# Twenty-four value rows gathered as half rows, and the last gate layer split by input half

## The chip, the core and the metric

The kernel runs on one core of a Trainium2 chip. It is one program with one instruction stream for each engine: TensorE (PE, and PEld for its weight loads), VectorE (DVE), ScalarE (ACT), GpSimd (POOL) and the DMA queue of SyncE (SP). Engines wait for one another through semaphores. The metric is the device time of one execution in microseconds (us), as the median of several runs.

## What is computed

Two transformer blocks on 256 tokens of width 2048, in float32. The change lies at the very end of the second block: a feed-forward layer that looks up experts in a table, and after it a gate layer.

```
def peer_ffn(x, w_peer_q, peer_subkeys, peer_u, peer_v):
    ...                       # per token: 8 heads x 16 experts of 16384, softmax gates
    def chunk(args):          # 128 tokens
        xc, ec, gc = args
        u = peer_u[ec]
        act = jax.nn.gelu(jnp.einsum('tkd,td->tk', u, xc))
        return jnp.einsum('tk,tkd->td', gc * act, peer_v[ec])
...
    h = h + peer_ffn(rms_norm_2(h, ffn_norm[l]), ...)
    gate = jax.nn.sigmoid(rms_norm_2(h, ple_norm[l]) @ w_ple_gate[l])
    h = h + gate * (p[l] @ w_ple_proj[l])
return rms_norm_2(h, final_norm)
```

Each token needs 128 rows of `peer_u` and 128 rows of `peer_v`, 2048 floats each. For the 256 tokens that is 512 gathers, each of one row for 128 tokens (1 MiB).

## The kernel before

**Gathers.** The list `gathers` holds one entry for each transfer: `("u", n, k)` or `("v", n, k)`, where n is token half times 8 plus head (0 to 15) and k the expert (0 to 15). GpSimd issues them in this order as indirect DMAs (L640), each into one of ten row buffers `ROWS`: four in `BIG`, one in `HF`, five in `HLF`, which later hold the split weights of the gate layer. A gather waits until its buffer's last row was used (L629 to L633). The transfers number from q = 0 to 511; u rows run ahead of v rows, the last u row is q = 494.

**Use of a row.** VectorE takes every u row (a dot product with the normed input, L2730). Of the v rows TensorE takes three of four: ScalarE makes a diagonal matrix of the row's gates (`DIAG`), and TensorE multiplies it with the row's four blocks of 512 columns and sums in four banks. VectorE takes the fourth (multiply and add into `ACC`, L2750). Eight rows of the last head (n = 15, k from 8 on) are cut between them: VectorE takes the left 1024 columns (L2746), TensorE the right ones.

**From sums to the gate layer.** After the last row VectorE adds a bank into `ACC` (`joined`, 512 columns), TensorE turns that block (`turned_values`, four transposes), VectorE adds it to the residual X (`added`), ScalarE squares it (`half_square`) and makes the upper half of the normed input (four chunks of 128), and VectorE makes the lower half (`normed_low`). This goes block by block, four blocks of 512 columns for the second 128 tokens.

**The gate layer** `w2_pg` has 32 units of 512 KiB, two for each of 16 output chunks of 128 columns: one for the input's left 1024 columns, one for the right. A unit is loaded by SP into one of three `RAW` buffers, copied with rounding by ScalarE (`high`), and its remainder made by VectorE (`low`), into one of five `HLF` buffers; then TensorE makes 24 products of 256 columns. `RAW` is free again after `low`. For a finished chunk VectorE multiplies the bank with the row norm `RX` (`scaled`, into `GT`), ScalarE takes the sigmoid in place, VectorE multiplies with `PRJ` and adds to X, and ScalarE squares it and scales it for the output (`OUT`). There are three banks for the chunks.

VectorE's order in this layer is written out in its `dense`: for each unit `low(u + 3)`, and after a chunk's last unit the four steps above. Every engine works strictly in the order of its own stream.

Of the kernel before, what the change touches and what calls it, by code (L numbers as in the profile page):

```python
# [7 lines left out]
U32 = mybir.dt.uint32  # L8
# [35 lines left out]
          ("w2_pg", 16, 8, 128, 2, False)]  # L44
# [3 lines left out]
LATE = ("w_ck", "w_out", "w2_ao", "w2_pg")  # L48
# [140 lines left out]
def build(nc, A, out):  # L189
    ctx = ExitStack()  # L190
    with ctx:
# [9 lines left out]
        STREAM = [A[n[:5]][int(n[5:])] if n[:5] in ("w2_uk", "w2_uv") else A[n][b * a.parts + p]  # L201
# [132 lines left out]
        ROWS = [big(12288 + 2048 * i, 2048) for i in range(4)] + [HF[:, 0, 0:2048]] + [HLF[:, i, :] for i in range(NPAIR)]  # L334
        DIAG = [KEEP[:, i // 2, 128 * (i % 2):128 * (i % 2) + 128] for i in range(4)]
# [18 lines left out]
        us, vs = [[(x, n, k) for n in range(16) for k in range(16)] for x in ("u", "v")]  # L354
        gathers = []
        for a in range(256):
            gathers.append(us[a])
            while vs and a >= 16 * vs[0][1] + 17 and 256 - len(vs) < min((a - 17) * 240 / 238, (a - 39) * 1.6):
                gathers.append(vs.pop(0))
        gathers += vs  # L360
        taken = {g: q for q, g in enumerate(gathers)}

        def by_vector(g):
            return g[0] == "u" or g[2] % 4 == 3 or (g[1] == 15 and g[2] % 2 == 1)

        def halved(g):

            return g[0] == "v" and g[1] == 15 and g[2] >= 8

# [9 lines left out]
        last = [3, pair[2], pair[3], 4, 0, 1, 2, 3, pair[2], pair[3]]  # L379
        NG = len(gathers)  # L380

        def buffer(q):
            if q < 19:
                return first_rows[q]
            if q < 46:
                return beside_pq[(q - 19) % 9]
            return early[(q - 16) % 10] if q < NG - 10 else last[q - NG + 10]

        place, used, vturn, pturn, seen = [], [[] for _ in ROWS], [], [], [0, 0]
        for q, g in enumerate(gathers):  # L390
            b = buffer(q)
            place.append((b, len(used[b]) + 1, used[b][-1] if used[b] else None))
            used[b].append(q)
            seen[0] += not by_vector(g) or halved(g)
            seen[1] += by_vector(g) or halved(g)
# [3 lines left out]
        PG_FREE = max(used[b][-1] for b in (pair[4], pair[0], pair[1]))  # L399
# [10 lines left out]
        s_row = [sem(f"rows{i}_in") for i in range(5 + NPAIR)]  # L410
# [35 lines left out]
        s_sig, s_res = sem("ple_sigmoid"), sem("ple_added")  # L446
# [37 lines left out]
        PQ0, PP0, PG0 = L["w_pq"].unit0, L["w2_pp"].unit0, L["w2_pg"].unit0  # L484
# [79 lines left out]
        def gpsimd(e):  # L564
# [59 lines left out]
            for q, (table, n, k) in enumerate(gathers):  # L624
# [4 lines left out]
                if before is not None:  # L629
                    if by_vector(gathers[before]) or halved(gathers[before]):  # L630
                        e.wait_ge(s_vused, vturn[before])
                    if not by_vector(gathers[before]) or halved(gathers[before]):
                        e.wait_ge(s_pused, pturn[before])  # L633
# [4 lines left out]
                elif slot == 4:  # L638
                    e.wait_ge(s_mm, L["w_pq"].end())
                e.indirect_dma_start(out=ROWS[slot], out_offset=None, in_=A["peer_" + table],  # L640
# [7 lines left out]
        def tensor(e):  # L648
# [605 lines left out]
            def value(q, n, k, table="v"):  # L1254
# [13 lines left out]
                for b in range(2 if halved((table, n, k)) else 0, 4):  # L1268
                    end = 14 if i == 0 else 6 if b < 2 else 15
                    m = mm(PS[4 - 4 * i + b][:, :], DIAG[(p - 1) % 4], ROWS[slot][:, 512 * b:512 * b + 512], n % 8 + k == 0,  # L1270
                           n % 8 == 7 and k == end)
                m.then_inc(s_pused, 1)

            def turned_values(i, j):
                pe.wait_ge(s_acc, 4 * i + 4 if i == 0 else 5 + j)
                if i == 1 and j < 2:
# [14 lines left out]
            for q, (table, n, k) in enumerate(gathers):  # L1291
                if not by_vector(gathers[q]) or halved(gathers[q]):
                    value(q, n, k)
# [20 lines left out]
            dense(L["w2_pg"], normed("ple_norm"), None, None, later_sums)  # L1314
# [9 lines left out]
        def scalar(e):  # L1324
# [629 lines left out]
            for q, (table, n, k) in enumerate(gathers):  # L1954
# [6 lines left out]
                if not by_vector(gathers[q]) or halved(gathers[q]):  # L1961
# [7 lines left out]
                if q == PG_FREE + 5:  # L1969
                    s.wait_ge(s_vused, max(vturn[p] for p in range(PG_FREE + 1)))  # L1970
                    s.wait_ge(s_pused, max(pturn[p] for p in range(PG_FREE + 1)))
                    for j in range(3):
                        high(L["w2_pg"].unit0 + j)
            pg = L["w2_pg"]
            s.wait_ge(s_vused, VTURNS)
            s.wait_ge(s_pused, PTURNS)
            high(pg.unit0)
            high(pg.unit0 + 1)
            for j in range(4):
                if j == 2:  # L1980
                    high(pg.unit0 + 2)
# [8 lines left out]
            def evac_pg(c):  # L1990
                bank_done(L["w2_pg"], c)
# [7 lines left out]
            high(pg.unit0 + 3)  # L1999
            high(pg.unit0 + 4)  # L2000
            dense(pg, evac_pg)
# [5 lines left out]
        def vector(e):  # L2007
# [676 lines left out]
            def route(n):  # L2684
# [31 lines left out]
                ts(GA[:, i, 16 * h:16 * h + 16], BV, BV[:, 0:1], None, ALU.subtract)  # L2716
                copy(EX[:, i, 16 * h:16 * h + 16], I12[:, 0:16], (s_ext, n + 1))
# [22 lines left out]
            def value(q, n, k):  # L2740
# [3 lines left out]
                if halved(("v", n, k)):  # L2744
                    o = ACC[:, i, 0:1024]
                    v.done(e.scalar_tensor_tensor(out=o, in0=row[:, 0:1024], scalar=c, in1=o, op0=ALU.mult, op1=ALU.add), sig)  # L2746
# [6 lines left out]
            def joined(i, b):  # L2753

                v.wait_ge(s_pused, pturn[taken["v", 8 * i + 7, 14 if i == 0 else 6 if b < 2 else 15]])
                o = ACC[:, i, 512 * b:512 * b + 512]
                tt(o, o, PS[4 - 4 * i + b][:, :], ALU.add, (s_acc, 4 * i + b + 1))
# [244 lines left out]
```

## Time and profile before

| | |
|---|---|
| median of 3 runs | 3695.53 us (3695.16 to 3697.79) |
| profiled execution, its own time | 3696.61 us |
| its span, first to last instruction | 3694.8 us |
| busy: PE, DVE, ACT, POOL | 87%, 68%, 39%, 24% of the span |
| DMA moved | 952.30 MB, mean 258 GB/s |

The span is what the rows of the trace cover; the execution's own time is 1.8 us more, and the median of the runs 0.7 us more than the span. All times in rows count from the start of the span. The last gather lands in the last 120 us of the span, and everything the change touches lies in the last 200 us.

### The profile page before, as it was taken

The numbers are of one execution on the slowest core, as the hardware profiler recorded it, in microseconds if no ns is written. First come the engines' busy times: TensorE is split into PE (matmuls) and PEld (weight loads), VectorE is DVE, ScalarE is ACT, GpSimd is POOL, SyncE is SP. The second block draws the span as 40 slices with busy tenths as digits, with TensorE's granted clock in tenths as the row PEclk, the third lists the DMA queues.
The fourth block names the chain that finished last, engine by engine and source line by source line (L and its number), as shares of the span: only waits on it lengthen the run. The fifth ranks groups of instructions, "written<-read, shape, count | busy, mean of one in ns | idle before, by whom it ended". The sixth has DMA issues, their size and how long they took to land.

```text
span 3694.8 us, 44301 instructions
## 1 busy us (share of the span) xinstructions
PE 3200.4 (87%) x16462; PEld 2476.9 (67%) x16462; DVE 2496.8 (68%) x3435; ACT 1429.4 (39%) x2139; POOL 899.5 (24%) x624
## 2 busy tenths in 40 slices
PE   8998999999999999999999999677666666666678
PEld 7777878888888889998998888533222232222248
DVE  6578866665566567875647766966777786555566
ACT  6455655653355445565546551211100110100125
POOL 2000010000000100000000013565655566566522
PEclk9998999999999999999999999898988888878799
DMA  6433343556555555455553458999999999999974
GB/s 217 159 123 115 107 161 127 183 188 195 182 190 192 191 203 187 161 184 192 177 177 115 158 187 323 417 422 421 421 421 422 421 421 422 422 421 421 422 282 160
DMA packets 187879, 952.30 MB, mean 258 GB/s; under 512 B 20880, under 2 KB 21008, under 8 KB 121872
## 3 DMA queue, kind: packets, MB, share of 16 engines
q0 software_dynamic: 73728, 536.90, 35.0%
q1 hardware_dynamic: 113936, 412.56, 33.9%
q8 instruction: 131, 2.15, 0.2%
q14 instruction: 84, 0.69, 0.1%
HBM read 947.29 MB, written 2.10 MB: 257 GB/s over the span
## 4 chain that ended last, share of the span: by engine, by line
PE 57%; DMA 21%; DVE 14%; POOL 3%; ACT 3%; issue 2%; DVEq 0%; ACTq 0%; SPq 0%; POOLq 0%
PE ps L658 56%; DMA HLF<-in_peer_v,CS 9%; DMA BIG<-in_peer_v,CS 6%; DMA HLF<-in_peer_u,CS 3%; DVE HL L2027 2%; DVE HLF L2730 2%; DMA HF<-in_peer_v,CS 2%; DVE BIG L2031 1%; POOL BIG L640 1%; POOL HLF L640 1%; DVE BIG L2027 1%; DVE BIG L2730 1%; DMA BIG<-in_peer_u,CS 1%; ACT HL L1343 1%; DVE BIG L2023 1%
## 5 line engine op out<-in xcount | busy, mean ns | idle before, releaser
L658 PE MATMUL ps<-HS,HL 128*128 128x256 f32 (+1 forms) x7040 | 1110.2, 314 | 0.0
L2027 DVE TENSOR_TENSOR HL<-RAW,HL 128x1024 fp32r<-128x1024 f32 (+1 forms) x736 | 905.8, 1231 | 233.9 <-ACT HL L1343 175.2
L658 PEld LDWEIGHTS ps<-HS,HL 128*128 128x128 f32 x7040 | 992.9, 192 | 83.0 <-issue 2.9
L1343 ACT CAST HL<-RAW 128x1024 fp32r<-128x1024 f32 (+1 forms) x736 | 768.5, 1044 | 463.4 <-PE ps L658 178.7
L658 PE MATMUL ps<-BIGR,HL 128*128 128x256 f32 (+1 forms) x5376 | 888.7, 320 | 14.4 <-ACT HL L1343 9.5
L658 PEld LDWEIGHTS ps<-BIGR,HL 128*128 128x128 f32 x5376 | 779.4, 192 | 92.8 <-issue 11.7
L658 PE MATMUL ps<-HLF,KEEP 128*128 128x512 f32 x724 | 386.0, 687 | 193.4 <-DMA HLF<-in_peer_v,CS 177.0
L658 PE MATMUL ps<-BIG,KEEP 128*128 128x512 f32 x648 | 336.4, 672 | 164.2 <-DMA BIG<-in_peer_v,CS 126.4
L658 PEld LDWEIGHTS ps<-HLF,KEEP 128*128 128x128 f32 x724 | 155.1, 222 | 421.6 <-issue 353.9
L2730 DVE CUSTOM_DVE_ANT_0 HLF<-HLF,BIG 128x2048 f32<-128x2048 f32 x133 | 304.9, 2293 | 191.2 <-DMA HLF<-in_peer_u,CS 183.2
L658 PEld LDWEIGHTS ps<-BIG,KEEP 128*128 128x128 f32 x648 | 135.6, 217 | 360.0 <-issue 331.5
L1339 ACT ACTIVATE KEEP<-CON,GA 128x128 f32<-128x128 f32 x192 | 77.1, 402 | 729.4 <-PE ps L658 642.1
L576 POOL COPY NSUM<-TMP 128x256 f32<-128x256 f32 x5 | 3.5, 692 | 1459.3 <-ACT TMP L1339 1459.3
L2730 DVE CUSTOM_DVE_ANT_0 BIG<-BIG 128x2048 f32<-128x2048 f32 x97 | 222.4, 2293 | 117.4 <-DMA BIG<-in_peer_u,CS 110.8
L640 POOL DMA_INDIRECT HLF<-in_peer_u,CS x133 | 207.2, 1558 | 97.8 <-PE ps L658 49.4
L640 POOL DMA_INDIRECT HLF<-in_peer_v,CS x124 | 180.6, 1457 | 169.7 <-PE ps L658 124.6
L640 POOL DMA_INDIRECT BIG<-in_peer_v,CS x111 | 153.8, 1386 | 147.4 <-PE ps L658 116.7
L578 POOL TENSOR_TENSOR NSUM<-NSUM,TMP 128x256 f32<-128x256 f32 x74 | 92.3, 1248 | 344.0 <-ACT TMP L1339 342.9
L640 POOL DMA_INDIRECT BIG<-in_peer_u,CS x97 | 148.9, 1535 | 95.9 <-DVE CS L2035 33.4
L2027 DVE TENSOR_TENSOR X<-X,ps 128x256 f32<-128x256 f32 (+1 forms) x168 | 72.9, 434 | 143.1 <-PE ps L658 137.4
L658 PE MATMUL ps<-HL,HS 128*128 128x512 f32 x576 | 137.6, 396 | 0.2 <-ACT BIG L1339 0.2
L658 PEld LDWEIGHTS ps<-HL,HS 128*128 128x128 f32 x576 | 107.6, 190 | 25.0 <-issue 2.3
(219 smaller groups left out, 2550.5 us busy)
## 6 DMA issues: line engine op xcount, KB each, us to landing
RAW<-in_w_up SPq DMA_DIRECT2D x128, 512.0 KB, 3.5
RAW<-in_w_down SPq DMA_DIRECT2D x128, 512.0 KB, 4.2
RAW<-in_w_out SPq DMA_DIRECT2D x64, 512.0 KB, 3.4
RAW<-in_w_qk SPq DMA_DIRECT2D x32, 512.0 KB, 3.7
RAW<-in_w_xbc SPq DMA_DIRECT2D x32, 512.0 KB, 3.2
RAW<-in_w_xr SPq DMA_DIRECT2D x32, 512.0 KB, 3.4
RAW<-in_w_yr SPq DMA_DIRECT2D x32, 512.0 KB, 3.3
RAW<-in_w_gr SPq DMA_DIRECT2D x32, 512.0 KB, 3.9
```

Of the source, the lines that this page charges most:

```text
L576: g.done(e.tensor_copy(NSUM[:, :], sq[:, 0, :]), sig)
L578: g.done(e.tensor_tensor(NSUM[:, :], NSUM[:, :], sq[:, j, :], ALU.add), sig)
L640: e.indirect_dma_start(out=ROWS[slot], out_offset=None, in_=A["peer_" + table], in_offset=bass.IndirectOffsetOnAxis(ap=EX[:, i, 16 * h + k ...
L658: return e.matmul(o, l, r, start=start, stop=stop, skip_group_check=True)
L1339: s.done(e.activation(o, i, f, bias=bias, scale=scale), sig)
L1343: s.done(e.copy(o, i), sig)
L2023: v.done(e.tensor_scalar(o, i, s1, s2, op0, op1), sig)
L2027: v.done(e.tensor_tensor(o, a, b, op), sig)
L2031: v.done(e.scalar_tensor_tensor(out=o, in0=a, scalar=s, in1=b, op0=op0, op1=op1), sig)
L2730: v.done(e.tensor_tensor_reduce(row, row, HN[:, i, :], 1.0, 0.0, ALU.mult, ALU.add, DOT[:, i, 16 * h + k:16 * h + k + 1]), sig)
```

## The change

The 24 v rows (n = 14, k from 8) and (n = 15, all k) are no longer gathered whole. They leave the list of whole rows, which then ends at q = 487, and follow it as 24 left halves ("l", 512 KiB each) and then 24 right halves ("r"). The index of a half row is twice the expert's, plus one for a right half; VectorE makes both lists in the routing step (four small operations for each of two heads). The halves go into ten half buffers, two in each of the four `BIG` rows and the `HF` row, in turn. TensorE takes the left halves with even k and VectorE the others; VectorE takes all right halves.

The gate layer becomes two layers of 16 units, `w2_pg0` (left inputs) and `w2_pg1` (right inputs). `w2_pg0` starts when the left half of X is complete; ScalarE copies its 16 results into `GSUM`. VectorE meanwhile adds right halves and makes lows by turns. When all right halves are added, the right half of X is completed, and `w2_pg1` runs. For each chunk VectorE now adds bank and `GSUM`, multiplies with `RX`, and goes on as before.

```
-          ("w2_pg", 16, 8, 128, 2, False)]
+          ("w2_pg0", 16, 8, 128, 1, False), ("w2_pg1", 16, 8, 128, 1, False)]
...
+        split = [(n, k) for n in (14, 15) for k in range(16) if n == 15 or k >= 8]
+        vs = [x for x in vs if x[1:] not in split]
...
+        NF = len(gathers)
+        gathers += [(x, n, k) for x in ("l", "r") for n, k in split]
...
+            if q < NF:
+                return early[(q - 16) % 10]
+            return 10 + 2 * ((q - NF) % 5) + (q - NF) // 5 % 2
```

On TensorE:

```
-            for j in range(4):
-                turned_values(1, j)
-            half_sum(1, 0)
-            half_sum(1, 1)
+            turned_values(1, 0)
+            turned_values(1, 1)
...
-            dense(L["w2_pg"], normed("ple_norm"), None, None, later_sums)
+            gated = normed("ple_norm")
+            dense(L["w2_pg0"], gated, None, None, first_sums)
+            turned_values(1, 2)
+            turned_values(1, 3)
+            dense(L["w2_pg1"], lambda k: gated(k + 8), None, None, later_sums)
```

On ScalarE:

```
+            def evac_first(c):
+                s.wait_ge(s_mm, L["w2_pg0"].done(c))
+                copy(GSUM[:, c, :], bank(L["w2_pg0"], c)[:, 0:T], sig_bank(L["w2_pg0"], c))
+
+            gate_high(0)
+            gate_high(1)
+            dense(L["w2_pg0"], evac_first)
+            gate_high(2)
+            gate_high(3)
```

On VectorE:

```
-            joined(1, 2)
+            joined(1, 0)
             added(1, 0)
-            joined(1, 3)
+            joined(1, 1)
             added(1, 1)
-            low(pg)
             normed_lows(0)
+            normed_lows(1)
+            for r, (n, k) in enumerate(split):
+                value(taken["r", n, k], n, k, "r")
+                while made[0] <= PG0 + 4 + (2 * r + 2) // 3 and made[0] < PG0 + 19:
+                    low(made[0])
             added(1, 2)
-            normed_lows(1)
-            low(pg + 1)
+            normed_lows(2)
             added(1, 3)
...
             def evac_pg(c):
-                scaled(GT[:, :], L["w2_pg"], c)
+                v.wait_ge(s_mm, L["w2_pg1"].done(c))
+                bank_done(L["w2_pg0"], c)
+                tt(GT[:, :], bank(L["w2_pg1"], c)[:, 0:T], GSUM[:, c, :], ALU.add, sig_bank(L["w2_pg1"], c))
+                tt(GT[:, :], GT[:, :], RX, ALU.mult, (s_gs, c + 1))
                 v.wait_ge(s_sig, c + 1)
```

Three places show how the instructions stand. On GpSimd, at the end of the list of gathers, before:

```order
L640 DMA HLF<-in_peer_u,CS1 128x2048
L640 DMA HLF<-in_peer_v,CS1 128x2048
L640 DMA HF<-in_peer_v,CS1 128x2048
L640 DMA HLF<-in_peer_v,CS1 128x2048
L640 DMA BIG<-in_peer_v,CS1 128x2048 x2
```

and now:

```order
L648 DMA HLF<-in_peer_u,CS1 128x2048 x2
L648 DMA HF<-in_peer_u,CS1 128x2048
L648 DMA HLF<-in_peer_u,CS1 128x2048
L644 DMA BIG<-in_peer_v,SM 128x1024 x4
L644 DMA HF<-in_peer_v,SM 128x1024
```

The last whole rows are now u rows, which VectorE alone takes; the half rows follow, the fifth of them into the `HF` buffer that the last but one whole row leaves.

On VectorE, between the sums of the second token half and the gate layer, before (`HL<-RAW,HL` is a low, `HF<-HF,ps` a join, `X<-X,ps` an addition to the residual, `BIGR<-X,VEC,BIGR` lower halves of the normed input):

```order
L2027 TENSOR_TENSOR HF<-HF,ps 128x512
L2027 TENSOR_TENSOR X<-X,ps 128x4x128
L2031 SCALAR_TENSOR_TENSOR BIGR<-X,VEC,BIGR 128x256 x8
L2027 TENSOR_TENSOR HL<-RAW,HL 128x1024
L2039 RECIPROCAL KEEP<-KEEP 128x256
```

and now, with the loop over right halves (`HF<-BIG,GA,HF`) between the two halves of X:

```order
L2051 SCALAR_TENSOR_TENSOR BIGR<-X,VEC,BIGR 128x256 x8
L2771 SCALAR_TENSOR_TENSOR HF<-HF,GA 128x1024
L2771 SCALAR_TENSOR_TENSOR HF<-BIG,GA,HF 128x1024
L2047 TENSOR_TENSOR HL<-RAW,HL 128x1024
L2771 SCALAR_TENSOR_TENSOR HF<-BIG,GA,HF 128x1024 x3
L2047 TENSOR_TENSOR X<-X,ps 128x4x128
L2051 SCALAR_TENSOR_TENSOR BIGR<-X,VEC,BIGR 128x256 x4
L2059 RECIPROCAL KEEP<-KEEP 128x256
```

24 half-row operations and 14 lows stand in that loop.

On TensorE, from the last row on, before:

```order
L658 MATMUL ps<-HLF,KEEP 128x512 x4
L662 MATMUL ps<-CON,HF 128x128 x16
L658 MATMUL ps<-TMP,CON 128x128 x8
L658 MATMUL ps<-BIGR,HL 128x256 x24
L658 MATMUL ps<-BIGR,HL 128x256 x744
```

and now:

```order
L666 MATMUL ps<-BIG,KEEP 128x512 x8
L670 MATMUL ps<-CON,HF 128x128 x8
L666 MATMUL ps<-BIGR,HL 128x256 x24
L666 MATMUL ps<-TMP,CON 128x128 x8
L666 MATMUL ps<-BIGR,HL 128x256 x360
```

The products of the gate layer are 768 as before; eight of the sixteen transposes now stand between two halves of 384.

## Rows read from the trace of the kernel before

**Rows 1.** Chain that ended last: start us, us, what.

```profile
3559.78 17.09 DMA HLF<-in_peer_v,CS
...
3590.04 90.44 PE ps L658 x752
```

**Rows 2.** Windows: length, busy time (instructions) of each engine, PEclk, DMA share, GB/s.

```profile
3510.00:3520.00 10.00, 3.74 (x9) 1.50 (x10) 6.96 (x5) 2.41 (x4) 6.88 (x5) 0.88 1.02 423
...
3620.00:3640.00 20.00, 20.00 (x169) 20.00 (x169) 13.81 (x19) 13.10 (x19) 5.37 (x4) 1.00 0.57 189
```

**Rows 3.** Timeline, arrivals: start us, us, engine, instruction, idle time and its releaser.

```profile
3512.24 2.29 DVE L2730 CUSTOM_DVE_ANT_0 HF<-HF,BIG 128x2048 f32<-128x2048 f32 x1 [2.67 <-DMA HF<-in_peer_u,CS]
...
3514.74 2.35 DVE L2750 SCALAR_TENSOR_TENSOR HF<-HLF,GA,HF 128x2048 f32<-128x2048 f32 x1 [0.20 <-DMA HLF<-in_peer_v,CS]
...
3573.30 1.96 PE L658 MATMUL ps<-HLF,KEEP 128*128 128x512 f32 x4 [1.46 <-DMA HLF<-in_peer_v,CS]
...
3577.01 1.95 PE L658 MATMUL ps<-HLF,KEEP 128*128 128x512 f32 x4 [1.76 <-DMA HLF<-in_peer_v,CS]
```

**Rows 4.** Timeline, GpSimd's issues: the first gather, then two late ones.

```profile
2259.65 1.19 POOL L640 DMA_INDIRECT BIG<-in_peer_u,CS  x1 [26.90 <-DVE CS L2035]
...
2265.40 2.29 DVE L2730 CUSTOM_DVE_ANT_0 BIG<-BIG 128x2048 f32<-128x2048 f32 x1 [6.68 <-DMA BIG<-in_peer_u,CS]
...
3444.85 0.94 POOL L640 DMA_INDIRECT HLF<-in_peer_v,CS  x1 [3.77 <-PE ps L658]
...
3456.61 2.29 DVE L2730 CUSTOM_DVE_ANT_0 HLF<-HLF,BIG 128x2048 f32<-128x2048 f32 x1
3457.58 2.13 POOL L640 DMA_INDIRECT BIG<-in_peer_v,CS  x1 [0.30 <-issue]
```

**Rows 5.** Timeline, VectorE's half rows and lows.

```profile
3563.28 1.23 DVE L2027 TENSOR_TENSOR HL<-RAW,HL 128x1024 fp32r<-128x1024 f32 x1
...
3564.61 1.28 DVE L2746 SCALAR_TENSOR_TENSOR HF<-BIG,GA,HF 128x1024 f32<-128x1024 f32 x1
3565.99 1.41 DVE L2027 TENSOR_TENSOR HF<-HF,ps 128x512 f32<-128x512 f32 x2
```

**Rows 6.** DMA issues, 3500 to 3577: count, size, median us from issue to landing.

```profile
RAW<-in_w_pg SPq DMA_DIRECT2D x3, 512.0 KB, 7.5
```

**Rows 7.** Timeline, from the last sums to the row norm.

```profile
3579.80 0.69 DVE L2027 TENSOR_TENSOR X<-X,ps 128x512 f32<-128x512 f32 x1
...
3580.63 0.63 PE L662 MATMUL ps<-CON,HF 128*128 128x128 f32 x4 [0.79 <-DVE X L2027]
3580.66 0.63 ACT L1339 ACTIVATE TMP<-X 128x512 f32<-128x512 f32 x1 [13.79 <-DVE X L2027]
...
3581.32 2.13 ACT L1339 ACTIVATE BIGR<-X,VEC 128x256 fp32r<-128x256 f32 x4
...
3593.55 0.48 ACT L1339 ACTIVATE KEEP<-ps,CON 128x256 f32<-128x256 f32 x1
...
3596.53 1.75 DVE L2039 RECIPROCAL KEEP<-KEEP 128x256 f32<-128x256 f32 x1
```

**Rows 8.** Timeline, gate layer: one chunk on VectorE, then the last two chunks.

```profile
3617.44 0.42 DVE L2027 TENSOR_TENSOR GT<-ps,KEEP 128x256 f32<-128x256 f32 x1
...
3618.35 0.42 DVE L2027 TENSOR_TENSOR BIG<-BIG,GT 128x256 f32<-128x256 f32 x1 [0.48 <-ACT GT L1339]
3618.81 0.43 DVE L2027 TENSOR_TENSOR X<-X,BIG 128x256 f32<-128x256 f32 x1
...
3619.34 1.23 DVE L2027 TENSOR_TENSOR HL<-RAW,HL 128x1024 fp32r<-128x1024 f32 x1
...
3674.74 0.42 DVE L2027 TENSOR_TENSOR GT<-ps,KEEP 128x256 f32<-128x256 f32 x1 [1.11 <-PE ps L658]
...
3680.51 0.42 DVE L2027 TENSOR_TENSOR GT<-ps,KEEP 128x256 f32<-128x256 f32 x1 [3.97 <-PE ps L658]
...
3681.87 0.42 DVE L2027 TENSOR_TENSOR X<-X,BIG 128x256 f32<-128x256 f32 x1
```

More of the change, by code:

```diff
@@ L334, in build @@
         ROWS = [big(12288 + 2048 * i, 2048) for i in range(4)] + [HF[:, 0, 0:2048]] + [HLF[:, i, :] for i in range(NPAIR)]
+        ROWS += [ROWS[s][:, 1024 * j:1024 * j + 1024] for s in range(5) for j in range(2)]
+        EXH = SM[:, 448:512].bitcast(U32).rearrange("p (h k) -> p h k", h=2)
+        HALVES = A["peer_v"].rearrange("n (h d) -> (n h) d", h=2)
+        GSUM = HF[:, :, :].rearrange("p a b -> p (a b)")[:, 2048:6144].rearrange("p (c t) -> p c t", t=T)
         DIAG = [KEEP[:, i // 2, 128 * (i % 2):128 * (i % 2) + 128] for i in range(4)]
@@ L409, in build @@
         s_sk, s_p = sem("subkeys_in"), sem("p_in")
-        s_row = [sem(f"rows{i}_in") for i in range(5 + NPAIR)]
+        s_row = [sem(f"rows{i}_in") for i in range(15 + NPAIR)]
         s_store = [sem(f"out{i}_stored") for i in range(4)]
@@ L629, in gpsimd @@
                 if before is not None:
-                    if by_vector(gathers[before]) or halved(gathers[before]):
+                    if by_vector(gathers[before]):
                         e.wait_ge(s_vused, vturn[before])
-                    if not by_vector(gathers[before]) or halved(gathers[before]):
+                    else:
                         e.wait_ge(s_pused, pturn[before])
@@ L1291, in tensor @@
             for q, (table, n, k) in enumerate(gathers):
-                if not by_vector(gathers[q]) or halved(gathers[q]):
-                    value(q, n, k)
+                if not by_vector(gathers[q]):
+                    value(q, n, k, table)
                 if q == HALF0 + 8:
@@ L1972, in scalar, with gate_high @@
                     for j in range(3):
-                        high(L["w2_pg"].unit0 + j)
-            pg = L["w2_pg"]
-            s.wait_ge(s_vused, VTURNS)
-            s.wait_ge(s_pused, PTURNS)
[L1977 to L1981, printed above, removed]
+                        high(PG0 + j)
+                if q == PG_FREE + 16:
+                    high(PG0 + 3)
+                    high(PG0 + 4)
+            s.wait_ge(s_vused, vturn[taken["u", 15, 15]])
+            s.wait_ge(s_pused, PTURNS)
+            def gate_high(j):
                 half_square(1, j)
@@ L2743, in value @@
                 c = GA[:, i, 16 * h + k:16 * h + k + 1]
-                if halved(("v", n, k)):
-                    o = ACC[:, i, 0:1024]
-                    v.done(e.scalar_tensor_tensor(out=o, in0=row[:, 0:1024], scalar=c, in1=o, op0=ALU.mult, op1=ALU.add), sig)
+                if table != "v":
+                    o = ACC[:, i, 1024:2048] if table == "r" else ACC[:, i, 0:1024]
+                    v.done(e.scalar_tensor_tensor(out=o, in0=row, scalar=c, in1=o, op0=ALU.mult, op1=ALU.add), sig)
                 elif h == 0 and k == 3:
```

86 lines of the change are left out of this document (46 added, 40 removed).

## The prediction

> **What bounds the kernel now.** I read the chain that ended last first. Its end is two stretches: transfers of value rows up to 3559.78 + 17.09 = 3576.87, and TensorE's gate layer from 3590.04 for 90.4 us [rows 1]. So 118 us of the span of 3694.8 lie behind the last landing. The windows then tell what limits each stretch. While rows are gathered the DMA engines are full (share 1.02 at 423 GB/s), so a row of 1.049 MB takes 2.48 us; TensorE and VectorE wait. In the gate layer TensorE is busy without a break, at a granted clock of 1.00, and DMA is at 0.57 [rows 2]. The two stretches use different things, and the change lets 12 rows' worth of bytes move beside half of the layer's products. The timeline then tells what the steps cost, and who waits there.
>
> **The time up to the last left half.** Up to q = 487 the same 488 MiB are gathered, in nearly the same order. In the trace of before row 487 arrives at 3514.7 [rows 3]. The last eight whole rows are now all VectorE's; 2.29 us each plus about 0.1 fits into 2.48, so I keep 3514.7. From there before needs 62.2 us for 24 rows. Now there are 24 halves of 1.24 us, 29.8 us, and three or four raw blocks of the gate layer among them, which cost about 1.25 us each (3577.01 − 3573.30 = 3.71 us for a row and, by the excess, a block) [rows 3].
>
> Two things slow this down. The fifth half needs the `HF` buffer, thus row 486, whose dot product ends at about 3514.5 (as the one at 3512.24 + 2.29 does) [rows 3]. By then VectorE begins the next. An issue on GpSimd takes 0.94 us when VectorE is idle, but the one that began at 3457.58 during a dot product ended 0.8 us after that product's end (3459.71 against 3458.90), then 0.30 to the next [rows 4]. So the fifth half is issued by 3517.9. The first gather landed 4.5 us after its issue ended (2265.40 against 2260.84), of which 2.5 are the transfer [rows 4]; a half needs 2.0 + 1.25 = 3.3 us, and lands at 3521.2. Then 19 halves and 4 blocks at 1.25 to 1.27 give 29 us by DMA. GpSimd's pace lies between 1.24 (never blocked) and about 1.8 (always blocked; half a VectorE instruction, 0.8 and 0.30); VectorE has 12 halves, 5 lows and 2 joins there, 24.6 us or three quarters of the time, so I take 1.6, 30.4 us. They run beside each other: the last left half lands at **3551.5**, 25.4 us before the 3576.9 of now. All at DMA's pace, without the wait for row 486, would be 3548; always blocked 3555.
>
> **Left sums to the layer's first half: 10.1 us.** TensorE's or VectorE's last row and a join 2.1, turning 0.65, addition to X 0.74, then on ScalarE a square and four scalings, twice, 0.17 + 2 × 2.89, and a last lower half on VectorE 0.6 [rows 7]. At **3561.6** VectorE enters its loop. TensorE finishes its first unit about 1.1 us later.
>
> **The loop.** On VectorE a half row takes 1.38 us from start to start (3565.99 − 3564.61), a low 1.33 (3564.61 − 3563.28) [rows 5]. 24 × 1.38 + 14 × 1.33 = 51.7 us. TensorE needs 5.77 us for a chunk of two units (3680.51 − 3674.74) [rows 8], 2.88 for one, and is done 15 × 2.88 = 43.3 us after its first: at 3606. So VectorE ends this stretch, not TensorE or DMA. The transfers are hidden: ten right halves can land before VectorE wants the first, later ones are asked for one by one every 2.2 us. What stands behind a waiting low is every right half after it: a low waits for ScalarE's high, that for its block. A buffer of three is freed by the low three before, 10.1 us earlier at this pace; 7.5 us of landing under load [rows 6] and some 1.1 of the high leave 1.5 spare. I add 1 us: the loop ends at **3614.3**, and TensorE has been idle for 8 us.
>
> **Joint between the halves: 18.0 us** to chunk 0's addition to X. Turning and first addition 1.6; square and scalings 2.9; lower halves 0.6; second addition, which stands behind those, 0.75; 2.9; 0.6: 9.4 us [rows 7]. The rest of TensorE's first unit, some 10 products, 1.2 to 2.4 (after idle time it may run at the lower clock); norm sums 1.1; root 0.6; reciprocal 1.85 [rows 7]: to 14.8 with the middle of these. Then a low, 1.33, and from the first of four steps to the last 0.46 + 0.46 + 0.45 + 0.46 [rows 8]. At **3632.3** chunk 0 is added.
>
> **Second half.** Before, VectorE has three steps for a chunk: 3617.44, 3618.35 (after the sigmoid), 3618.81, and the next low at 3619.34 [rows 8]. Now four steps for each unit, all in series through `GT`: 0.46 + 0.46 + 0.45 + 0.46 + 0.53 (to the low) + 1.33 = 3.69 us, against TensorE's 2.88. Lows remain for 12 of the 15 chunks that follow (13 in all, one already counted); without a low 2.36. 12 × 3.69 + 3 × 2.36 = 51.4: the last addition starts at **3683.7**. VectorE is the bound here too; TensorE's work is covered.
>
> **End and sum.** From the last addition (3681.87 [rows 8]) to the end 12.9 us, which the change doesn't touch. 3551.5 + 10.1 + 52.7 + 18.0 + 51.4 + 12.9 = 3696.6, 1.8 us over the span of before. The profiled execution's own time is 3696.61; the median of the runs, 1.1 below it, is what I add 1.8 to: **3697.5 us**. So 25.4 us are won at the front and given back as a joint and as VectorE's extra work (24 right halves, 16 more steps). The routing's eight small operations cost nothing, as VectorE waits for rows there; without that cover 1 to 2 us. ScalarE's 16 copies of `GSUM` (under 0.5 us) lie in the first half, where it has one high per 2.88 us.
>
> **A rule on size, and a row.** The trace shows 2.0 us of a gather's landing that are no transfer [rows 4], and rows that still come every 2.48 us [rows 2], because several are in flight. The Trainium skill (DMA: Bandwidth & Descriptors, Anatomy of one DMA — SWDGE (gpsimd) path) gives the same fixed 2 us per DMA and, in its rules, asks for 1 MiB at least. Taken as time that is paid for each of 24 more DMAs, the rule speaks against this change by 48 us; by the row it is hidden while ten buffers are cycled, and rival (b) bounds what is left.
>
> **Rivals.** (a) *VectorE isn't the bound*: its steps overlap more than the rows say, and TensorE's 2.88 sets both halves. Then the first half ends 8 us and the last 51.4 − 15 × 2.88 = 8 us earlier: 3681. For it: TensorE never pauses in the layer now. Against: the extra instructions all stand on VectorE, and `GT` is one buffer. Half of this is 3689.5, just the bound of what can be measured.
> (b) *Half rows cost more than half*, slower: 4 KiB pieces may be less efficient. The gate layer's blocks have such pieces: 189 GB/s at a share of 0.57 is 332 for a full share, against 415 for rows [rows 2]. A half would take 1.58 us instead of 1.25; 24 halves and 4 blocks, 9 us: 3706.5. It decides from about 1.5 us on. The low share may only be latency at each block's start, so this is the upper bound.
> (c) *Raw blocks starve the loop*, slower: three buffers cycle in 7.5 + 1.1 + 1.33 and a half row that the low has to sit out, 1.38, 11.3 us, 3.77 per unit against 3.37, over 14 units 5.6 us; with 8.5 us of landing 10. 3703 to 3708.
>
> **How the numbers follow.** A run of this kernel tells 0.2% (7.4 us) from no change. Forecast 0.60, its own range 3691 to 3703; (a) 0.14; (b) 0.16; (c) 0.10. A fast outcome needs (a) nearly whole: faster 0.14, same 0.60, slower 0.26. The range goes from (a)'s half, 3688, to (b) or (c) with some of the other, 3710.
>
> **What would show it.** Last left half at 3549 to 3555; VectorE without a gap over 1 us in the loop of 24 right halves and 14 lows, about 52 us long; TensorE idle for some 8 us before eight transposes, then a joint of 18 us; in the second half chunks every 3.7 us on VectorE, TensorE pausing once a chunk. Wrong would be: a landing spacing of halves over 1.5 us, lows that wait for highs, or chunks at 2.9 us.

## The result and the profile after

The changed kernel takes 3711.39 us, the median of 7 runs (3709.35 to 3713.54); the kernel before took 3695.89 beside it. The ratio is 1.0039, its 95% interval 1.0028 to 1.0051. The forecast was 3697.5 (3688 to 3710) and "same": the change costs 15.5 us where 2 were expected, and the interval lies clear of 1. The profiled execution has a span of 3708.3 against 3694.8. I follow that span through the prediction's terms.

Windows of the changed kernel: the loop, the joint, the second half (columns as in [rows 2]).

```profile
3590.00:3612.00 22.00, 21.59 (x180) 21.39 (x179) 20.33 (x17) 9.97 (x14) 7.54 (x5) 1.00 0.86 319
3620.00:3634.00 14.00, 10.54 (x44) 9.41 (x43) 5.25 (x10) 5.33 (x10) 0.00 (x0) 0.50 0.00 1
3640.00:3660.00 20.00, 17.09 (x135) 16.13 (x134) 15.64 (x29) 12.38 (x21) 6.60 (x5) 1.00 0.45 143
```

Before, TensorE was busy for all of its 20 us at a clock of 1.00 [rows 2]. Now the joint's first 14 us run at 0.50, which is the lower of its two levels, and in the second half TensorE is idle for 2.9 of 20 us.

The end of the chain that ended last:

```profile
3528.04 11.09 DMA BIG<-in_peer_v,SM
...
3627.51 15.89 PE ps L666 x104
```

The last long wait for a transfer has moved forward, but TensorE's 90 us without a break [rows 1] are gone. Timeline, from the issues of half rows to the end of the loop:

```profile
3506.73 3.02 POOL L644 DMA_INDIRECT BIG<-in_peer_v,SM  x1 [1.97 <-DVE CS L2755]
3514.15 2.98 POOL L644 DMA_INDIRECT HF<-in_peer_v,SM  x1 [4.39 <-DVE CS L2755]
...
3549.51 1.96 PE L666 MATMUL ps<-BIG,KEEP 128*128 128x512 f32 x4 [0.22 <-DMA BIG<-in_peer_v,SM]
3552.07 1.96 PE L666 MATMUL ps<-BIG,KEEP 128*128 128x512 f32 x4 [0.61 <-DMA BIG<-in_peer_v,SM]
3554.19 1.28 DVE L2771 SCALAR_TENSOR_TENSOR HF<-BIG,GA,HF 128x1024 f32<-128x1024 f32 x1 [0.90 <-DMA BIG<-in_peer_v,SM]
...
3564.87 1.28 DVE L2771 SCALAR_TENSOR_TENSOR HF<-HF,GA 128x1024 f32<-128x1024 f32 x1
...
3616.88 2.68 DVE L2771 SCALAR_TENSOR_TENSOR HF<-BIG,GA,HF 128x1024 f32<-128x1024 f32 x2
3619.61 1.97 PE L670 MATMUL ps<-CON,HF 128*128 128x128 f32 x8 [8.02 <-DVE HF L2771]
```

Towards the end TensorE, which takes every other left half, gets one each 2.56 us, so a half costs 1.28. The last is there at 3554.2, 22.7 us ahead of the last row before (3576.87) [rows 1]. VectorE's loop runs from 3564.9 to 3619.6, and TensorE has then waited 8.0 us. In the loop VectorE waited little; its longest wait from 3564 to 3620 (total, times, longest):

```profile
DVE HL L2047 <- ACT HL L1356: 2.7, 2, 2.0
```

These are lows that wait for highs. The joint:

```profile
3627.51 4.27 PE L666 MATMUL ps<-BIGR,HL 128*128 128x256 f32 x16 [1.71 <-DVE BIGR L2051]
3631.57 3.06 PE L666 MATMUL ps<-TMP,CON 128*128 128x128 f32 x16
3634.70 1.28 ACT L1352 ACT_TABLE_LOAD   x1 [6.14 <-PE ps L666]
3635.99 0.47 ACT L1352 ACTIVATE KEEP<-ps,CON 128x256 f32<-128x256 f32 x1
3636.50 1.75 DVE L2059 RECIPROCAL KEEP<-KEEP 128x256 f32<-128x256 f32 x1 [7.28 <-ACT KEEP L1352]
...
3639.72 0.42 DVE L2047 TENSOR_TENSOR GT<-ps,HF 128x256 f32<-128x256 f32 x1
...
3641.55 0.42 DVE L2047 TENSOR_TENSOR X<-X,BIG 128x256 f32<-128x256 f32 x1
```

One thing stands behind another: rest of the unit, 16 products of the norm sums, a table load on ScalarE, root, reciprocal, low. Chunk 0 is added at 3641.55. The second half and its end:

```profile
3643.41 0.42 DVE L2047 TENSOR_TENSOR GT<-ps,HF 128x256 f32<-128x256 f32 x1
...
3647.09 0.42 DVE L2047 TENSOR_TENSOR GT<-ps,HF 128x256 f32<-128x256 f32 x1
...
3682.98 1.22 DVE L2047 TENSOR_TENSOR HL<-RAW,HL 128x1024 fp32r<-128x1024 f32 x1
3683.40 1.38 POOL L580 TENSOR_TENSOR NSUM<-NSUM,TMP 128x256 f32<-128x256 f32 x1 [2.30 <-ACT TMP L1352]
...
3687.09 0.74 POOL L580 TENSOR_TENSOR NSUM<-NSUM,TMP 128x256 f32<-128x256 f32 x1 [2.31 <-ACT TMP L1352]
3687.12 0.99 DVE L2047 TENSOR_TENSOR GT<-GT,KEEP 128x256 f32<-128x256 f32 x1
...
3694.85 0.43 DVE L2047 TENSOR_TENSOR X<-X,BIG 128x256 f32<-128x256 f32 x1
```

From chunk to chunk 3.68 us, as forecast (3.69); the two POOL rows and what they collide with come up at the end. In a table:

| term | forecast, us | measured, us | more |
|---|---|---|---|
| last left half | 3551.5 | 3554.2 | 2.7 |
| to the loop | 10.1 | 10.7 | 0.6 |
| the loop | 52.7 | 54.7 | 2.0 |
| joint, to chunk 0's addition to X | 18.0 | 22.0 | 4.0 |
| second half, to the last addition | 51.4 | 53.3 | 1.9 |
| end | 12.9 | 13.4 | 0.5 |

Together 11.7 us, the span's 3708.3 against 3696.6. The median lies 3.1 above this span, where I had counted on 0.9: the profiled execution's own time was 3710.29, 2.0 above its span and 1.1 below the median.

### The profile page after: what moved, and what is told of

Its sections match the earlier page's. It is cut to its first block, busy times and chain, and to the rows that moved or that the text cites. A ratio compares the mean times of both kernels' runs of the same rounds, so it can differ in the third digit from the quotient of the medians.

```text
span 3708.3 us, 44289 instructions
## 1 busy us (share of the span) xinstructions
PE 3181.4 (86%) x16398; PEld 2471.9 (67%) x16398; DVE 2527.8 (68%) x3481; ACT 1433.2 (39%) x2149; POOL 928.0 (25%) x648
## 4 chain that ended last, share of the span: by engine, by line
PE 55%; DMA 20%; DVE 16%; POOL 4%; ACT 2%; issue 2%; DVEq 0%; ACTq 0%; SPq 0%; POOLq 0%
PE ps L666 54%; DMA HLF<-in_peer_v,CS 9%; DMA BIG<-in_peer_v,CS 5%; DVE HL L2047 3%; DMA HLF<-in_peer_u,CS 3%; DVE HLF L2755 2%; POOL BIG L648 1%; DVE BIG L2051 1%; DVE BIG L2047 1%; POOL HLF L648 1%; DVE BIG L2755 1%; DVE HF L2771 1%; DMA BIG<-in_peer_u,CS 1%; DMA HF<-in_peer_v,CS 1%; DMA HF<-in_peer_u,CS 1%
## 5 line engine op out<-in xcount | busy, mean ns | idle before, releaser
L666 PE MATMUL ps<-BIGR,HL 128*128 128x256 f32 (+1 forms) x5376 | 899.2, 322 | 27.0 <-ACT HL L1356 10.1
L666 PE MATMUL ps<-HLF,KEEP 128*128 128x512 f32 x696 | 373.3, 692 | 182.7 <-DMA HLF<-in_peer_v,CS 156.3
L666 PE MATMUL ps<-BIG,KEEP 128*128 128x512 f32 x616 | 325.9, 682 | 184.9 <-DMA BIG<-in_peer_v,CS 125.6
L648 POOL DMA_INDIRECT HLF<-in_peer_v,CS x115 | 168.4, 1464 | 166.2 <-PE ps L666 122.4
L648 POOL DMA_INDIRECT BIG<-in_peer_v,CS x98 | 136.8, 1395 | 131.3 <-PE ps L666 105.6
```

Source lines behind the costliest of these rows:

```text
L666: return e.matmul(o, l, r, start=start, stop=stop, skip_group_check=True)
```

## The experiments

The last two columns are against the kernel before on the same chip.

| run | median, us | above before | ratio, 95% interval |
|---|---|---|---|
| the changed kernel | 3711.39 | 15.5 | 1.0028 to 1.0051 |
| layer_split | 3708.11 | 10.4 | 1.0018 to 1.0039 |
| halves_only | 3704.69 | 7.5 | 1.0012 to 1.0030 |
| no_right | 3701.30 | 3.6 | 1.0002 to 1.0021 |
| rows16 | 3710.53 | 13.7 | 1.0026 to 1.0054 |
| warm | 3713.53 | 15.8 | 1.0030 to 1.0058 |
| early_sums | 3706.59 | 9.4 | 1.0017 to 1.0037 |
| root_ready | 3709.30 | 12.1 | 1.0023 to 1.0050 |
| two_gates | 3705.95 | 8.3 | 1.0013 to 1.0031 |
| joint_all | 3701.57 | 4.4 | 1.0006 to 1.0024 |
| hidden16 | 3710.74 | 13.9 | 1.0029 to 1.0056 |
| hidden12 | 3720.39 | 23.6 | 1.0050 to 1.0077 |
| drawn16 | 3707.25 | 10.6 | 1.0017 to 1.0041 |
| drawn12 | 3709.88 | 13.3 | 1.0022 to 1.0049 |
| drawn_lows | 3697.35 | 0.3 | 0.9992 to 1.0010 |
| drawn_root | 3693.35 | -4.3 | 0.9981 to 0.9999 |

### The two parts of the change, each alone

**layer_split**: the kernel before with the gate layer's new order alone.

```
-          ("w2_pg", 16, 8, 128, 2, False)]
+          ("w2_pg0", 16, 8, 128, 1, False), ("w2_pg1", 16, 8, 128, 1, False)]
...
+                tt(GT[:, :], bank(L["w2_pg1"], c)[:, 0:T], GSUM[:, c, :], ALU.add, sig_bank(L["w2_pg1"], c))
+                tt(GT[:, :], GT[:, :], RX, ALU.mult, (s_gs, c + 1))
```

> The kernel before, value rows whole as they were, with only the gate layer's order changed: the left halves of all 16 units first, their sums kept in GSUM, then the right halves with the fourth step on VectorE. Theory (the fourth step makes VectorE the bound of the second half, 3.69 us for a chunk against TensorE's 2.88): 12 chunks of 0.81 us more, the time 8 to 10 us above the kernel before, 3704 to 3706. Rival (the extra step is hidden behind TensorE, and the change loses in its joint and its loop alone): within 2 us of the kernel before.

10.4 us more. Its timeline, the first step of two chunks:

```profile
3650.26 0.42 DVE L2036 TENSOR_TENSOR GT<-ps,HF 128x256 f32<-128x256 f32 x1
...
3653.95 0.42 DVE L2036 TENSOR_TENSOR GT<-ps,HF 128x256 f32<-128x256 f32 x1
```

3.69 us a chunk, without any half row in the kernel: the layer's new order has this price by itself. It isn't shown to be the fourth step's alone. All four steps now stand behind each unit of the second half, where three stood behind two units, and they pass through one `GT`. With three steps behind each unit the sum would be 3.69 − 0.46 = 3.23 us, an estimate from [rows 8], still above TensorE's 2.88.

**halves_only**: the kernel before with the last 24 value rows each fetched in two transfers.

```
+                if (table, n, k) in split:
+                    col = 16 * (n - 14) + k
+                    for side in range(2):
+                        e.indirect_dma_start(out=ROWS[slot][:, 1024 * side:1024 * side + 1024], out_offset=None, in_=HALVES,
+                                             in_offset=bass.IndirectOffsetOnAxis(ap=EXH[:, side, col:col + 1], axis=0)
+                                             ).then_inc(s_row[slot], 16)
```

> The kernel before with its last 24 value rows each fetched by two transfers of half a row into the same buffer, and nothing else changed but the indices for them. Theory (a half costs half: they land every 1.24 to 1.28 us in the changed kernel too): within 2 us of the kernel before. Rival (24 more transfers cost their fixed part or GpSimd's issue, 1.6 to 2 us a half): 8 to 18 us more.

7.5 us more: just under the rival's 8 to 18. Its timeline, a row on VectorE, two issues beside and behind it, and the last half row; then a window (columns as in [rows 2]):

```profile
3541.04 2.35 DVE L2765 SCALAR_TENSOR_TENSOR HF<-HLF,GA,HF 128x2048 f32<-128x2048 f32 x1 [2.14 <-DMA HLF<-in_peer_v,SM]
3541.26 2.95 POOL L646 DMA_INDIRECT HLF<-in_peer_v,SM  x1 [0.30 <-issue]
3544.51 0.94 POOL L646 DMA_INDIRECT BIG<-in_peer_v,SM  x1 [0.30 <-issue]
...
3585.69 1.28 DVE L2761 SCALAR_TENSOR_TENSOR HF<-HLF,GA,HF 128x1024 f32<-128x1024 f32 x1 [3.06 <-DMA HLF<-in_peer_v,SM]
```

```profile
3540.00:3560.00 20.00, 17.34 (x31) 6.71 (x29) 8.46 (x4) 4.34 (x6) 16.32 (x13) 0.81 0.85 279
```

The last half comes at 3585.7, 8.7 us after the last row before [rows 3]. An issue that begins while VectorE works on a row ends 0.8 us after that row (2.95 us); alone it takes 0.94. With two issues a row GpSimd can't keep a pace of 1.25 us, and the DMA share falls to 0.85. So I read the price, 0.3 us for each of 24 more transfers, as one of issues; the run doesn't part it from other costs of a transfer. In bytes a half costs nearly what half a row does: 1.28 us at a full DMA share in the changed kernel, against 1.24.

**no_right**: the changed kernel without the right halves.

```
-        gathers += [(x, n, k) for x in ("l", "r") for n, k in split]
+        gathers += [("l", n, k) for n, k in split]
...
-                value(taken["r", n, k], n, k, "r")
```

> The changed kernel without the 24 right half rows: neither gathered nor added, so the last 24 value rows count with their left halves alone. Theory (VectorE's 24 right halves and 14 lows set the first half's 54.7 us): the first half is now TensorE's, 15 units of 2.88 us, 44 to 46 us; TensorE isn't idle before the joint, so that its clock stays up and the joint is 18 to 19 us; in all 11 to 14 us below the changed kernel's, 3697 to 3700. Rival (the raw blocks' cycle sets the first half): the lows still come every 3.5 us or more, and it stays above 50 us.

3701.3 against 3697 to 3700 expected; 11.9 less than the changed kernel, each against its own before. Its timeline, TensorE in the first half, the transposes behind it and the rest of the unit in the joint:

```profile
3567.36 43.44 PE L666 MATMUL ps<-BIGR,HL 128*128 128x256 f32 x360
3610.63 1.03 PE L670 MATMUL ps<-CON,HF 128*128 128x128 f32 x8
...
3618.01 4.27 PE L666 MATMUL ps<-BIGR,HL 128*128 128x256 f32 x16 [2.01 <-DVE BIGR L2051]
```

15 units in 43.4 us without a gap, as forecast for a first half that TensorE sets. The run also takes 24 transfers off the DMA engines (share 0.53 instead of 0.86 from 3590 to 3612), so by itself it doesn't part VectorE from the raw blocks. The waits above do: of the 54.7 us VectorE spent 2.7 on lows that waited for highs, and a chain of raw blocks could claim no more. But the joint, from the transposes to chunk 0's addition at 3631.46, is still 20.8 us, though TensorE wasn't idle ahead of it. I had expected 18 to 19.

**rows16**: 16 half rows instead of 24.

```
-        split = [(n, k) for n in (14, 15) for k in range(16) if n == 15 or k >= 8]
+        split = [(15, k) for k in range(16)]
```

> The changed kernel with the last 16 value rows in halves instead of the last 24, the 14 lows spread over 16 right halves. Theory (with 24, VectorE's loop of 54.7 us is longer than TensorE's 15 units, 43.3; each half row less gives back 1.25 us at the front and takes 1.38 off the loop until TensorE sets it): the last left half lands 8 to 10 us later, the loop is 45 to 47 us, TensorE is idle for under 2 us before the joint; the time is 0 to 2 us below the changed kernel's. Rival (the gain at the front is the larger part, the loop is set by raw blocks): 5 us or more above it.

1.8 us less, each against its own before. VectorE enters the loop at 3574.0, 9.2 us later, and ends it at 3620.0 (46.0 us instead of 54.7); TensorE's 15 units take the same 43.4 us. What the front loses, the loop gives back: between 16 and 24 the number of half rows isn't what decides.

### The joint

**warm**: products of no use on TensorE ahead of and in the joint.

```
+                if k == 4 and not begun_late[0]:
+                    begun_late[0] = True
+                    busy(12)
...
+            busy(56)
             turned_values(1, 2)
             turned_values(1, 3)
...
+            busy(10)
```

> The changed kernel with products of no use on TensorE (56 ahead of the second half's transposes, 10 behind them, 12 ahead of the last four sections of chunk 0), so that it isn't idle for the 8.0 us before the joint. Theory (the joint took 22.0 us where 18.0 were forecast since TensorE, idle before, ran it at a granted clock of 0.50): the clock in the joint is above 0.8, the joint about 18.5 us, the time 3 to 4 us below the changed kernel's, 3707.5 to 3708.5 as a median. Rival (the joint is long by its waits on VectorE and ScalarE, or the clock falls whatever TensorE does there): the joint stays at 21 to 23 us, the time within 1 us of the changed kernel's.

No change in the time, and yet the clock did what the theory says. Windows, then timeline:

```profile
3612.00:3620.00 8.00, 8.00 (x75) 8.00 (x74) 4.63 (x4) 0.00 (x0) 0.00 (x0) 1.00 0.30 105
3620.00:3634.00 14.00, 13.68 (x110) 12.57 (x109) 5.26 (x10) 5.53 (x11) 0.00 (x0) 1.00 0.00 1
```

```profile
3608.82 12.67 PE L666 MATMUL ps<-CON 128*128 128x128 f32 x112
...
3612.89 4.06 DVE L2785 SCALAR_TENSOR_TENSOR HF<-BIG,GA,HF 128x1024 f32<-128x1024 f32 x3
...
3621.33 1.04 PE L670 MATMUL ps<-CON,HF 128*128 128x128 f32 x8
...
3640.64 0.43 DVE L2061 TENSOR_TENSOR X<-X,BIG 128x256 f32<-128x256 f32 x1
```

The clock is 1.00 where it was 0.50. From the transposes to chunk 0's addition it takes 19.3 us instead of 21.9 (3641.55 - 3619.61), so the clock is worth up to 2.6 us. But the 56 products became 112 and ran for 12.7 us, 4.4 beyond the loop's end at 3616.95: what the clock gave, their length took. So the time says nothing here. The rows show the clock as one part of the joint's excess.

**early_sums**: the norm sums ahead of the unit's last four sections.

```
+                if k == 4 and not summed[0]:
+                    summed[0] = True
+                    half_sum(1, 2)
+                    half_sum(1, 3)
```

> The changed kernel with the last two norm sums (16 products) moved on TensorE from behind chunk 0's second-half unit to ahead of its last four sections, where TensorE waits for VectorE anyway. Theory (the joint's end is the chain unit, norm sums, root's table and root, reciprocal, low; the sums and what follows them needn't wait for the unit): chunk 0's first step on VectorE comes 4.5 to 6 us earlier after the transposes, the joint takes 16 to 17.5 us instead of 22.0, the time is 4 to 6 us below the changed kernel's. Rival (the joint is long by TensorE's low clock alone, so the unit ends late wherever the sums stand): below 2 us.

6.1 us less, each against its own before. Its timeline, after a loop that ended at 3622.1:

```profile
3628.11 2.75 PE L666 MATMUL ps<-TMP,CON 128*128 128x128 f32 x16
...
3631.18 1.28 ACT L1357 ACT_TABLE_LOAD   x1
...
3636.20 0.42 DVE L2052 TENSOR_TENSOR GT<-ps,HF 128x256 f32<-128x256 f32 x1
```

VectorE's first step comes 14.1 us after the loop instead of 20.1 (3639.72 - 3619.57). The joint is 15.9 us long: of the three changes to the joint, the place of the sums took out the most.

**root_ready**: the root's table loaded ahead.

```
             gate_high(3)
+            warm()
```

> The changed kernel with one root of one column on ScalarE behind the last scaling of the joint, so that the table of the root is loaded while the norm sums are still to come. Theory (the load of 1.28 us stands on the joint's path, which the forecast's term left out): the joint is 1.3 us shorter, 20.7 us, the time about 1.3 us below the changed kernel's, at the edge of what five rounds tell. Rival (the load is hidden by VectorE's work): no change in the joint.

The load moves to 3629.0, ahead of the end of the sums, and the joint goes from 22.0 to 20.6 us (loop's end at 3620.0, addition at 3640.55), as expected; in time 3.4 less, with intervals too wide for 1.3.

**two_gates**: two gate buffers.

```
-                tt(GT[:, :], GT[:, :], RX, ALU.mult, (s_gs, c + 1))
...
+                tt(g, g, RX, ALU.mult, (s_gs, c + 1))
+                if c:
+                    added_gate(c - 1)
```

> The changed kernel with two gate buffers in turn instead of one, so that VectorE adds and scales chunk c before it comes back to the sigmoid of chunk c - 1. Theory (in the second half VectorE's four steps in series through one buffer, with their waits for the sigmoid, set 3.69 us for a chunk): the waits of about 0.45 us go, a chunk takes 3.2 to 3.3 us, the time is 5 to 7 us below the changed kernel's, about 3705. Rival (VectorE's work itself or the arrival of raw blocks sets 3.69): within 1 us of the changed kernel's.

7.2 us less, each against its own before. A chunk takes 3.31 us now, and VectorE waits for nothing in it. So of the 0.81 us by which 3.69 exceeds TensorE's 2.88, 0.38 were waits through the one buffer and 0.43 are VectorE's work:

```profile
3644.72 0.42 DVE L2049 TENSOR_TENSOR GT<-ps,HF 128x256 f32<-128x256 f32 x1
...
3648.03 0.42 DVE L2049 TENSOR_TENSOR RS<-ps,HF 128x256 f32<-128x256 f32 x1
```

**joint_all**: the last three together.

> The changed kernel with two gate buffers, the norm sums moved ahead and the root's table loaded early, all three together. Theory (the three are on different stretches of one chain and add up): 7 + 5 + 1.3 = 12 to 15 us below the changed kernel's, 3697 to 3700, within 0.2% of the kernel before. Rival (what one shortens another bound takes back, the unit of chunk 0 or TensorE's 3.1 us for a chunk): 8 to 10 us.

11.1 us less, each against its own before: between theory and rival. The early table load adds nothing here. With the sums early ScalarE loads the table right behind its last scaling anyway (3631.18 above), and VectorE's first step comes 14.4 us after the loop, no sooner than in early_sums. Two of the three add up; still 4.4 above the kernel before.

### Drawing the joint into the first half

**hidden16** and **hidden12**: two gate buffers, 16 or 12 half rows, the right sums turned ahead of unit 12 or 9.

```
+                if used_left[0] == 16 * 12:
+                    turned_values(1, 2)
+                    turned_values(1, 3)
+                if used_left[0] == 16 * 15:
+                    half_sum(1, 2)
+                    half_sum(1, 3)
```

> The kernel with two gate buffers, with the last 16 value rows in halves, and with the joint drawn into the first half: the right sums are turned ahead of unit 12 of 16, their norm sums stand ahead of unit 15, the root comes on ScalarE before its last copy. Theory (the joint's 20 us cost what they do since TensorE waits in them; behind four units of 2.88 us they cost nothing, and the loop is TensorE's 46 us): from the changed kernel 7 us by the two gate buffers, 14 by the joint, 0 to 2 by the rows: 3687 to 3692, 5 to 10 us below the kernel before. Rival (the joint's additions and lows on VectorE delay the lows that TensorE needs, or the right halves aren't all in by unit 12, so TensorE waits inside the first half as long as it did behind it): 3697 or more.

> As the one with 16 rows and the joint drawn in, with 12 rows in halves and the right sums turned ahead of unit 9. Theory (four half rows less cost 5 us at the front and bring nothing, as TensorE already sets the loop): 3691 to 3697, some 4 to 5 us above the one with 16. Rival (with 16 the joint isn't hidden whole, with 12 it is): at or below the one with 16.

Both theories fell, hidden16 by 19 us. The first step of the second half came 72 us after the loop's start (3644.66), and TensorE waited for lows inside the first half: the rival. ScalarE's next high stood ahead of the scalings and waited 4.9 us for a raw block; that block's buffer is freed by a low which stood behind those scalings on VectorE.

**drawn16** and **drawn12** put the scalings ahead of the next highs.

> As the one with 16 half rows and the joint drawn into the first half, with its waits unwound: on ScalarE the squares and scalings of the right sums stand ahead of the next highs, on VectorE both additions stand ahead of the scalings' lower halves, and the first low comes after three right halves. Theory (there TensorE waited 1.8 to 4.8 us at five places because a high stood ahead of the scalings, waiting for a raw block whose buffer a low behind those scalings frees; the joint itself can be hidden): TensorE waits under 3 us in all between the first unit and the second half, whose first step on VectorE comes some 55 us after the loop's start instead of 72; the time is 3690 to 3695, 2 to 7 us below the kernel before. Rival (the joint's work on VectorE and ScalarE beside one low and one high per unit is itself more than TensorE's four units cover): 3698 or more.

> The same with 12 half rows and the right sums turned ahead of unit 9. Theory: four half rows less bring the left sums 5 us later and nothing else, 3695 to 3700. Rival (three units less than four are enough to hide the joint only with 12): at or below the one with 16.

The wait had only moved. Timeline of drawn16:

```profile
3610.61 1.48 DVE L2060 TENSOR_TENSOR X<-X,ps 128x512 f32<-128x512 f32 x2 [3.97 <-PE ps L671]
...
3616.71 1.04 ACT L1363 CAST HL<-RAW 128x1024 fp32r<-128x1024 f32 x1 [6.68 <-DMA RAW<-in_w_pg]
...
3623.17 5.75 PE L667 MATMUL ps<-BIGR,HL 128*128 128x256 f32 x32 [6.55 <-DVE HL L2060]
```

VectorE idles for 4.0 us ahead of the additions with the freeing low behind them. The runs with 12 rows can't tell what the number of rows does: their TensorE also waited 11 to 12 us ahead of its last left rows, for diagonals that stood behind highs on ScalarE.

**drawn_lows** does three lows ahead of the additions; **drawn_root** two more ahead of the reciprocal.

```
+            while made[0] <= PG0 + 14:
+                low(made[0])
             added(1, 2)
             added(1, 3)
```

> As drawn16, with the next three lows on VectorE ahead of the additions of the right sums instead of behind them. In drawn16 VectorE stood idle for 4.0 us ahead of the additions while the low that frees the next raw block's buffer stood behind them; ScalarE's high then waited 6.7 us for that block, and the scalings behind the high, so that TensorE waited 6.6 us. Theory (the joint can be hidden once no low stands behind what waits for a later high): these waits go, the first step of the second half comes at 54 to 58 us after the loop's start instead of 67, the time is 3694 to 3699, level with the kernel before. Rival (VectorE and ScalarE are simply full in these units): 3704 or more.

> As drawn_lows, with the last two lows of the stretch ahead of the reciprocal of the root instead of behind it. Theory (in drawn_lows VectorE is idle for 3.9 us ahead of the reciprocal and then does three lows, 3.9 us, while chunk 0 is ready): the second half starts 2.5 to 3.5 us earlier, the time is 3693 to 3696, 0 to 4 us below the kernel before, under 0.1% and so not to be told from it. Rival (those lows' highs come later than the root, so that the reciprocal waits for them): no change from drawn_lows or 1 to 2 us more.

Timeline of drawn_lows:

```profile
3609.59 8.87 PE L667 MATMUL ps<-BIGR,HL 128*128 128x256 f32 x72
...
3629.81 0.42 DVE L2060 TENSOR_TENSOR GT<-ps,HF 128x256 f32<-128x256 f32 x1
```

56.5 us after the loop's start at 3573.33, and 0.3 us above the kernel before. Window of drawn_root over the end of the first half, the joint and the start of the second:

```profile
3578.00:3630.00 52.00, 51.31 (x430) 51.13 (x429) 44.35 (x43) 30.36 (x45) 7.00 (x5) 1.00 0.62 209
```

TensorE is busy for 51.3 of 52 us at a clock of 1.00; there is no joint left to see. The time is 3693.35, 0.1% below the kernel before (ratio 0.9990, interval 0.9981 to 0.9999). It is the only one of 16 versions below it, by less than the 0.2% that I called measurable, and its interval only just leaves out 1: about level, perhaps a little faster.

## Why the prediction was wrong

**The step that failed is the joint: 18.0 us forecast, 22.0 measured.** It is the largest miss of six terms, which all came out longer. Its mechanism was right, its size was off, in three places of the sum: the norm sums took 3.1 us instead of 1.1 (3631.57 to 3634.63), the root with what precedes it 1.8 instead of 0.6, and the rest of the unit 2.4 instead of 1.8. The other steps are 0.3 longer together. Timeline of the kernel before:

```profile
3582.61 1.06 PE L658 MATMUL ps<-TMP,CON 128*128 128x128 f32 x8
...
3592.26 1.28 ACT L1339 ACT_TABLE_LOAD   x1
```

"Norm sums 1.1" is the length of one block of 8 products; here 16 stand behind the unit, at half clock. "Root 0.6" took the activation from [rows 7] and left out the table load that precedes it; before it lay beside TensorE's unbroken work, here it is on the path (root_ready). And I gave the lower clock to the rest of one unit; it held from the transposes through the norm sums (0.50), worth up to 2.6 us by the rows of warm. That idle time ahead of the joint is the cause of the low clock isn't shown: in no_right TensorE worked up to the transposes and its unit in the joint still took 4.27 us. The waits inside the joint are enough.

That the sums stand behind the unit was in the forecast. early_sums shows what this place costs, 6 us of the joint: no part of the miss, but a gain that I hadn't looked for.

**The front, 2.7 us late.** The fifth half landed at 3520.4 (6.2 us after its issue at 3514.15), 0.8 ahead of the forecast. The 19 halves behind it and their blocks took 33.8 us instead of 30.4. Windows of the changed kernel over that time:

```profile
3520.00:3540.00 20.00, 12.27 (x23) 4.43 (x22) 10.49 (x10) 6.37 (x11) 15.67 (x15) 0.84 0.97 357
3540.00:3555.00 15.00, 13.20 (x24) 4.87 (x22) 9.68 (x8) 0.80 (x2) 10.21 (x10) 0.83 1.03 410
```

The issues of 3.0 us in the rows above stand beside dot products, and the last of these ended at 3516.3, so they aren't the reason. From 3521.4 to 3540.2 GpSimd issued a half every 1.34 us, faster than the pace of 1.6 that I took. The first five of the 19 landed 1.9 us apart, over the 1.5 that I had named as a sign of being wrong; the next three, with three raw blocks among them, took 9.0 us at a DMA share of about 1.0; the later ones mostly came every 1.28. So from about 3524 on the DMA engines were the limit, and up to 3540 they moved 357 GB/s instead of the 410 behind it. How the 3.4 us divide between slow issues at the start (two of 1.7 us beside VectorE's half rows) and the raw blocks isn't shown. Rival (b) doesn't fit: where the DMA engines are full and mostly halves move, a half takes 1.28 us, not 1.58.

In the six other runs with 24 half rows the last left half came 38.6 to 39.6 us after the last u row, 40.2 in the profiled run of the changed kernel; 36.8 was forecast. So 1.8 to 2.8 us belong to the change and 0.6 to 1.6 to that execution, for a reason that isn't shown. The last u row itself came 0.7 us early.

**The loop, 2.0 us long.** VectorE set it, as forecast (no_right, rows16). My 1 us for waiting was 2.7 us of lows behind highs; rival (c) is that, at less than half its size (5.6 to 10 us).

**The second half** has the period I worked out, 3.69, and layer_split shows that the layer's new order costs 10 us by itself. What I missed are the last three chunks, 2.90 instead of 2.36 us, below. The 0.6 us up to the loop and the 0.5 at the end weren't followed up. The last step of the sum also has a slip: 3695.53 + 1.8 is 3697.3, not 3697.5.

**The rule on size.** The Trainium skill (DMA: Bandwidth & Descriptors, Anatomy of one DMA — SWDGE (gpsimd) path) gives a fixed 2 us per transfer. Taken as paid for each of 24 more, an estimate from it is 48 us; halves_only measures 7.5. So it doesn't hold as a sum, but I dropped it too easily: a transfer has a price that isn't bytes, and GpSimd's 0.94 to 3.0 us for the issue is the part of it that the rows show.

The missed terms of the joint have much in common: their durations came from rows where the same work ran at the full clock or beside other work, and the norm sums were counted by half. The gain at the front came nearly as forecast (22.7 us of 25.4). It went into the second half, with VectorE's four steps behind each unit (10 us by layer_split), into the loop, and into a joint in which every engine waits for another.

## What to carry to other kernels

Splitting a layer to start it early buys a joint: price it as a chain of single steps, with every table load, at the low clock, and look for what in it needn't stand where it does. A second gate buffer and the place of some instructions in the streams (in a kernel with 16 half rows instead of 24) decided here between 15.5 us lost and about level. When a wait is taken out, look for the buffer that is freed behind it: in drawn16 the wait had only moved a few instructions on.

## What was not expected of the hardware

In the last three chunks the multiplication `GT<-GT,KEEP` takes 0.99 us instead of 0.42, and the rows above show what it meets: GpSimd's addition began 0.03 us before it. 3.7 us earlier it was the other way round: VectorE's low began first, and GpSimd's addition took 1.38 us instead of 0.74. Without lows in the last chunks the two meet in every chunk, 3 × 0.55 us, in layer_split and two_gates as well. The Trainium skill (SBUF — State Buffer, Who interferes with whom) says that a VectorE instruction with both inputs in SBUF and a GpSimd instruction that reads SBUF exclude each other, and that the first to start goes through; these rows agree.

The issue of a gather is slowed beside VectorE too. In the changed kernel from 3480 us on, all 16 issues that began with VectorE idle took 0.94 us, and so did the 2 that began during a join, whose second input is a bank. Those that began during a dot product took up to 3.0, during a whole row's addition 2.2, during a half row's or a low up to 1.9.
